# Position bias of a selected-attention kernel: three parts as 48 columns, eighths of a key tile, most steps on ScalarE as plus/minus one

## The chip, the cores and the metric

The kernel runs on one core of a Trainium2 chip. The metric is the device time of one execution, in microseconds, from launch to end on that core. Below, PE is TensorE's matmul, PEld its weight load, DVE VectorE, ACT ScalarE, SP the SyncE queue. All sizes are for 512 tokens, in float32 unless said otherwise.

## What is computed

Two transformer blocks run back to back. The change touches one term of the first block's first attention branch, `dsa_attention`: the bias that is added to the scaled logits by the distance between a query and a key.

```python
def t5_bucket(dist):                       # 32 buckets
    d = jnp.maximum(dist, 0)
    dl = jnp.maximum(d, 16).astype(jnp.float32)
    large = 16 + (jnp.log(dl / 16) / math.log(128 / 16) * 16).astype(jnp.int32)
    return jnp.where(d < 16, d, jnp.minimum(large, 31))
...
bias = rel_bias[t5_bucket(pb[:, :, None] - p_sel)]      # rel_bias: 32 buckets x 4 heads
s = einsum('bthd,btkd->bthk', qb, k_sel) * scale + moveaxis(bias, -1, 2)
s = where(valid, s, -1e30); p = softmax(s)
```

The positions are inputs of the kernel. The 512 queries and 512 keys make a causal 4 x 4 grid of tiles of 128 x 128, of which ten are needed, each for four heads.

## The kernel before

**The whole.** The kernel is one program of some 19,800 instructions without loops on the device; each engine has its own stream, and semaphores tie the streams. In order: projections of the first block, an index score and a top-k selection, a gated recurrence, a latent attention (`mla`), the position bias, the selected attention (`dsa`), the output gates and projections, a feed-forward, and then the second block with its own projections, a state-space part and attention. Weights come through a ring of four slots on the SP queue. Most weight products are made as three float32r products (head by head, head by rest, rest by head; `triple`, L667 to L684), so each tile of weights is rounded by ACT (`weight_heads`, L1289) and its rest subtracted by DVE (`weight_rests`, L1634, called through `tt`, L1740).

**Work that is laid beside other work.** Projection products that nothing needs soon are cut in steps and spread over the stretches in which PE has gaps. `BESIDE` (L133) lists the steps, `PLACES` (L136) the places and how many steps each takes; PE, ACT and DVE each have a function `beside(place)` that runs the steps, drains the finished ones and prepares the coming weights. The last 24 tiles of `BESIDE` are the output gates: one tile is 8 x 3 matmuls of 512 columns, cut in two steps. ACT drains a finished gate tile by Tanh out of PSUM (`drains1`, L1403), and issues its DMA to DRAM on its own queue (L1404). Twelve places `bias 0` to `bias 11` take the last six steps, one in every other place, which are three gate tiles.

**The position bias.** A bucket's bias is a sum of increments: bias(d) is the sum over buckets b, up to the bucket of d, of `rel[b] - rel[b-1]`. So for a group of four keys the 32 bucket limits times 4 keys fill the 128 partitions; a **step** tile says for each (key, limit) and each query whether the query's position is at or past it (0 or 1), and a matmul with the step tile as weights and the increments as the moving operand (16 columns: 4 keys x 4 heads) gives the bias of 128 queries for 4 keys. The increments are split in three bfloat16 parts, `REL[0..2]`, whose products accumulate in PSUM, so that the sum has float32's precision. The steps are written as float32 and read as bfloat16 by taking every second half-word (`STEPS_B`, L417).

`BIAS_PARTS` (L422) goes by key tile: key tile 0 has four query tiles (and so 512 columns of steps), key tile 1 three, 2 two, 3 one. Within a key tile, for each of 32 groups of four keys:

- DVE makes the steps by one `is_ge` of 512, 384, 256 or 128 columns (L1998, recorded as L1743), at most four groups ahead of PE;
- PE makes, for each query tile, three matmuls of 16 columns (L976), each with its own weight load, into the query tile's own PSUM bank;
- after groups 7, 19 and 31 PE comes to a `beside` place.

When all 32 groups are done, DVE adds the mask `chosen` and writes the four heads' bias of each query tile to `BIAS` in SBUF (L2005, 512 columns each). The next key tile's matmuls wait for banks by `BIAS_FREE`. There are 128 DVE steps, 960 small matmuls and 10 of these additions. After the last, PE starts the scores of `dsa` (L815), DVE adds the bias to each score row (L2010) and takes its maximum, and ACT takes the exponential (L1270).

DVE's and ACT's helper `step` makes each instruction wait for the end of the one before.

## Time and profile before

| | |
|---|---|
| runs | 1639.21, 1639.64, 1646.55 us (median 1639.64) |
| the profiled execution | 1639.6 us |
| its span, first to last instruction | 1637.8 us |
| busy: PE / PEld / DVE / ACT / POOL | 1461.7 / 1117.3 / 966.7 / 479.3 / 16.2 us |
| mean granted clock of TensorE (1 is 2.4 GHz) | 0.935 |

The span is shorter than the time by what lies around it, 1.8 us. "Busy" of an engine counts its instructions' time; matmuls are pipelined, so a busy PE is not a PE at its peak. The granted clock is the share of 2.4 GHz that TensorE got; in a short stretch it is 1 or 0.5, and a mean between them says how the stretch was divided. In the groups of instructions a row gives the source line, the engine, the operation, the tiles (out<-in), shapes and count, then busy time in us, mean ns of one, and after the second bar the time for which the engine sat idle before them, with what ended that wait. Line numbers can be those of a helper: `ts` is L1743, `tt` L1740.

### The profile page before, as it was taken

What the parts mean: (1) busy time and instruction counts of PE and PEld (TensorE: products, weight loads), DVE (VectorE), ACT (ScalarE), POOL (GpSimd) and SP (SyncE); (2) the same over time, 40 slices, a digit from 0 to 9 for tenths busy, and PEclk for the clock granted to TensorE, in tenths of its full rate; (3) what the DMA queues carried; (4) which work ended last, traced back from release to release, by engine and by line L of the source; (5) the groups of instructions that cost most, each with busy time, mean ns of one, the idle gap of its engine ahead of it and who ended that gap; (6) DMA issues with size and microseconds to landing.
All of it is one profiled execution on the core that took longest, in us unless ns stands there. A gap on an engine that the chain in (4) does not pass through costs nothing.

```text
span 1637.8 us, 19815 instructions
## 1 busy us (share of the span) xinstructions
PE 1461.7 (89%) x7670; PEld 1117.3 (68%) x7670; DVE 966.7 (59%) x1649; ACT 479.3 (29%) x767; POOL 16.2 (1%) x11
## 2 busy tenths in 40 slices
PE   5998988896899888799899999999798997859998
PEld 4757888784577665687688888888477754446753
DVE  6259767655366767774546645533693648268840
ACT  5256322331322003323423432432213221114410
POOL 0000000000000000000000000000000011000000
PEclk9999999997999778899899999999898999969999
DMA  5112111221222100452134444123321112500001
GB/s 224 65 52 87 55 39 52 90 94 64 90 78 78 41 8 33 152 190 102 71 141 155 167 154 156 53 106 121 94 74 51 64 66 81 203 24 1 1 1 51
DMA packets 39885, 140.56 MB, mean 86 GB/s; under 512 B 13040, under 2 KB 17520, under 8 KB 27248
## 3 DMA queue, kind: packets, MB, share of 16 engines
q1 hardware_dynamic: 34608, 130.52, 22.2%
q10 hardware_dynamic: 5184, 8.78, 1.5%
q8 instruction: 61, 1.00, 0.2%
q14 instruction: 32, 0.26, 0.1%
HBM read 128.41 MB, written 8.39 MB: 84 GB/s over the span
## 4 chain that ended last, share of the span: by engine, by line
PE 53%; DVE 5%; issue 1%; ACT 1%; SPq 1%; DMA 0%; ACTq 0%; DVEq 0%; POOL 0%; POOLq 0%
PE turn L677 22%; PE score L662 7%; PE score L677 5%; PE sum L662 4%; PE turn L662 3%; PE sum L677 2%; PE sum L1205 2%; PE score L1110 1%; PE score L1179 1%; PE turn L1191 1%; SPq L603 1%; PE turn L1083 0%; DVE work L1740 0%; PE score L1236 0%; PE score L1150 0%
## 5 line engine op out<-in xcount | busy, mean ns | idle before, releaser
L1740 DVE TENSOR_TENSOR ring_r<-ring,heads_r 128x1024 fp32r<-128x1024 f32 (+3 forms) x153 | 176.3, 1152 | 216.8 <-ACT heads_r L1289 181.4
L1289 ACT ACTIVATE heads_r<-ring 128x1024 fp32r<-128x1024 f32 (+3 forms) x153 | 153.4, 1002 | 240.8 <-DMA ring<-wstream 103.1
L677 PE MATMUL score<-h_sb_r,heads_r 128*128 128x512 f32 x376 | 152.0, 404 | 0.0
L677 PE MATMUL turn<-tiles_r,heads_r 128*128 128x512 f32 x336 | 132.1, 393 | 0.0
L677 PE MATMUL turn<-h_sb_r,heads_r 128*128 128x512 f32 x304 | 119.5, 393 | 8.1 <-DVE ring_r L1740 8.1
L677 PE MATMUL turn<-wide_r,heads_r 128*128 128x512 f32 x312 | 121.9, 391 | 0.0
L677 PE MATMUL turn<-wide_r,ring_r 128*128 128x512 f32 x312 | 121.6, 390 | 0.0
L677 PE MATMUL score<-x_sb_r,heads_r 128*128 128x512 f32 x256 | 109.5, 428 | 8.2 <-DVE ring_r L1740 5.8
L677 PE MATMUL score<-x_sb_r,ring_r 128*128 128x512 f32 x256 | 104.3, 407 | 0.0
L677 PEld LDWEIGHTS score<-h_sb_r,heads_r 128*128 128x128 f32 x376 | 74.3, 197 | 14.7 <-issue 0.2
L677 PEld LDWEIGHTS turn<-tiles_r,heads_r 128*128 128x128 f32 x336 | 63.9, 190 | 13.3
L677 PEld LDWEIGHTS turn<-h_sb_r,heads_r 128*128 128x128 f32 x304 | 57.7, 190 | 20.4 <-issue 8.4
L677 PEld LDWEIGHTS score<-x_sb_r,heads_r 128*128 128x128 f32 x256 | 51.8, 202 | 23.9 <-issue 10.0
L677 PE MATMUL sum<-h_sb_r,heads_r 128*128 128x512 f32 x168 | 67.6, 403 | 0.0
L677 PEld LDWEIGHTS turn<-wide_r,heads_r 128*128 128x128 f32 x312 | 58.9, 189 | 12.3
L677 PEld LDWEIGHTS turn<-wide_r,ring_r 128*128 128x128 f32 x312 | 58.8, 188 | 12.2
L1258 ACT ACTIVATE tiles<-score 128x512 f32<-128x512 f32 x39 | 24.3, 622 | 143.1 <-PE score L677 73.8
L1743 DVE TENSOR_SCALAR work<-prow,work 128x512 f32<-128x512 f32 (+3 forms) x128 | 49.5, 386 | 19.7 <-PE turn L976 6.2
L677 PEld LDWEIGHTS score<-x_sb_r,ring_r 128*128 128x128 f32 x256 | 51.1, 200 | 11.6
L662 PE MATMUL score<-h_sb,ring 128*128 128x512 f32 x128 | 55.8, 592 | 0.0
L677 PE MATMUL turn<-h_sb_r,ring_r 128*128 128x512 f32 x128 | 50.3, 393 | 0.0
L677 PE MATMUL score<-wide_r,heads_r 128*128 128x512 f32 x120 | 47.3, 394 | 2.6 <-DVE h_sb_r L1740 2.6
(398 smaller groups left out, 2912.0 us busy)
## 6 DMA issues: line engine op xcount, KB each, us to landing
ring<-wstream SPq DMA_DIRECT2D x95, 1024.0 KB, 4.9
ring<-wstream SPq DMA_DIRECT2D x16, 704.0 KB, 4.3
ring<-gated SPq DMA_DIRECT2D x6, 1024.0 KB, 7.0
gated<-tiles ACTq DMA_DIRECT2D x15, 256.0 KB, 2.7
gated<-probs ACTq DMA_DIRECT2D x9, 256.0 KB, 2.0
x_sb<-xT SPq DMA_DIRECT2D x4, 512.0 KB, 5.7
x_sb<-xT ACTq DMA_DIRECT2D x1, 2048.0 KB, 8.1
outT<-x_sb SPq DMA_DIRECT2D x1, 2048.0 KB, 6.3
```

The costliest lines, as they stand in the source:

```text
L603: sp.dma_start(tiles[32 * r:32 * r + 32, 14 * T:18 * T].rearrange("p (k a m) -> p k a m", k=4, a=STEP)[:, :, m, :], U4[32 * m:32 * m + 32, ...
L662: mm = pe.matmul(out, l, r, start=(i == 0), stop=(i == len(pairs) - 1))
L677: return pe.matmul(out, a, w, **k) if moving else pe.matmul(out, w, a, **k)
L1110: mm = pe.matmul(b[0:2 * NCMP, 0:256], CB[kv][:, 8 * i + l, :], w[:, l, :], start=(i + l == 0), stop=(8 * i + l == 31))
L1179: pe.matmul(PAIR[p % 2][:, e * T:e * T + cols], TL[r, 18 + j, n * P:(n + 1) * P], KT2[r, 2 * a_ + j // 2, 0:cols], start=True, stop=False)
L1191: mm = pe.transpose(b[:, j * P:(j + 1) * P], PROB(i)[:, j * P:(j + 1) * P], ident)
L1205: mm = pe.matmul(OUT[g][:, h % 4 * P:h % 4 * P + P], PROBT(i)[:, j * P:(j + 1) * P], R2[:, j, at_v:at_v + P], start=(j == 0), stop=(j == n))
L1258: step(act.activation(out, b, func, bias=bias, scale=scale), name, gemm_done)
L1289: step(act.activation(head_piece(p), chunk(name)[:, c:c + cols], ACT.Identity), f"head {p}")
L1740: step(dve.tensor_tensor(out, a, b, op), name)
L1743: step(dve.tensor_scalar(out, a, s1, s2, o1, *([o2] if o2 is not None else [])), name)
```

## The change

The bias is cut in 32 **eighths** (`EIGHTHS`: key tile, eighth), four groups of four keys each, in the order of the key tiles.

- The three bfloat16 parts of the increments stand side by side in 48 columns. One matmul per step tile and query tile gives the three products, unsummed, in three places 64 columns apart of a PSUM bank. Two query tiles share a bank (192 of each 256 columns used); even eighths use the two `score` banks, odd ones the two `turn` banks. PE waits, before eighth i, for the additions of eighth i-2.
- Of each four groups, DVE makes the steps of the first as before; ACT makes the other three as Sign(position - limit + 0.5), plus or minus one, written as bfloat16 into a ring of eight tiles `SIGNS`. For these the increments are halved, with the last bucket's bias put to bucket 0 as the constant (`rel_last`, a new small input of 16 columns), so `REL` has two versions.
- DVE sums the three parts and the mask itself: for each pair of query tiles three dependent additions (`both` gives the view of two query tiles at once), 128 elements per partition for a pair, 64 for a single one.
- The increments' preparation, on DVE, goes from 10 to 18 small instructions, and a tile `KEYSIGN` is made of `KEYSTEP`, both ahead of them.
- The three gate tiles are cut into 24 steps of one k (three matmuls) each, one after each of the eighths 4 to 27. The places are six, at the eighths 4, 8, 12, 16, 20 and 24: there ACT drains finished gate tiles and rounds weights, and DVE subtracts rests.

```diff
@@ -135,7 +135,7 @@
          [("rows1_cq1", n) for n in range(NT)] + [(f"proj1c_{i // 4}", i) for i in range(4, 2 * len(PROJ1C))] + [(f"gate_{i // 4}", i) for i in range(2 * len(GATES))]
 PLACES = [(f"rank {i}", 2) for i in range(8)] + [(f"rec {h} {l}", 1) for h in range(4) for l in range(LEVELS + 1)] + \
          [(f"tail {i}", 2) for i in range(4)] + [("latent 0", 2), ("latent 1", 4)] + [(f"mla {i}", 1) for i in range(18)] + \
-         [(f"bias {i}", 1 - i % 2) for i in range(12)]
+         [(f"bias {i}", 1) for i in range(6)]
 PLACE = {n: i for i, (n, _) in enumerate(PLACES)}
 assert sum(k for _, k in PLACES) == len(BESIDE)
@@ -260,6 +260,10 @@
         for j in range(4):
             m[j, shift:, j, :] = a["rel_bias"][0:32 - shift]
         c[name] = m.reshape(P, 16)
+    m = np.zeros((4, 32, 4, 4), np.float32)
+    for j in range(4):
+        m[j, 0, j, :] = a["rel_bias"][31]
+    c["rel_last"] = m.reshape(P, 16)
     for kv in "kv":
         pos = a[f"cmp_pos_{kv}_2"][0].T
         c[f"pos_{kv}"] = np.concatenate([pos, pos], 0)
@@ -408,21 +412,33 @@
     BIAS = part(wide, 0, 5120, k=4)
     INDEX = [None] + [part(work, n * T, (n + 1) * P) for n in range(1, NT)]
     RANKED = [None, INDEX[1], INDEX[2], TL[:, 4, :]]
-    REL = [part(work, 6 * T + 8 * z, 8).bitcast(BF16) for z in range(3)]
-    KEYSTEP = part(work, 6 * T + 64, P)
-    def STEPS(g, cols):
-        return part(work, (2 + g % 4) * T, cols)
-    def STEPS_B(g, e):
-        return part(work, (2 + g % 4) * T + e * P, P).bitcast(BF16)[:, 1:2 * P:2]
-    BIAS_PARTS = [(0, (0, 1, 2, 3), (S[0], S[1], U[0], U[1])), (1, (1, 2, 3), (O[0], S[0], S[1])),
-                  (2, (2, 3), (U[0], U[1])), (3, (3,), (O[0],))]
-    BIAS_FREE = [0, 2, 4, 5]
+    REL = [part(work, 6 * T + 24 * v, 24).bitcast(BF16) for v in range(2)]
+    KEYSTEP, KEYSIGN = part(work, 6 * T + 64, P), part(work, 6 * T + 192, P)
+    STEP_OF = {g: ("act", "dve")[g % 4 == 0] for g in range(32)}
+    EIGHTHS = [(key, o) for key in range(NT) for o in range(8)]
+    BIAS_BANKS = [[S[0], S[1]], [U[0], U[1]]]
+    def STEPS(i):
+        return part(work, (2 + i % 2) * T, T)
+    def SIGNS(n):
+        return part(work, (7 * T, 4 * T)[n // 4 % 2] + n % 4 * 256, 256).bitcast(BF16)
+    def both(v, n, lo, count):
+        s = (n + 1) * P
+        x = max(0, lo + 2 * s - v.shape[-1])
+        if count == 1:
+            return v[:, :, lo:lo + 16].unsqueeze(1)
+        return v[:, :, lo - x:lo - x + 2 * s].rearrange("p h (e s) -> p e h s", e=2)[:, :, :, x:x + 16]
     LOGITS = [part(work, 4 * T, T), part(work, 5 * T, T)]
+    def signs_of(i, g):
+        return 3 * i + g % 4 - 1
     def upto(n):
@@ -692,7 +708,7 @@
                     at_c = c + k * P
                     last = any(c0 + k_ == at_c + P for _, c0, k_ in piece_of[name])
                     mm = triple(out, name, at_c, P, ah, ar, k == 0, k == n - 1, last)
-                    if halves and k == n // 2 - 1:
+                    if k < n - 1 and halves and (halves == "each" or k == n // 2 - 1):
                         yield
                 yield mm
@@ -706,7 +722,7 @@
                 for i, c in list(enumerate(by_twos(tiles_)))[first:last]:
                     for e in range(len(c)):
                         b = gemm_bank()
-                        for mm in split_tile(b[:, :], f"{tag}_{i}", e * KD * P, acts, None, True):
+                        for mm in split_tile(b[:, :], f"{tag}_{i}", e * KD * P, acts, None, "each" if tag == "gate" and 2 * i + e >= 21 else True):
                             if mm is None:
                                 yield
                         mm.then_inc(gemm_full, 1)
@@ -966,20 +982,24 @@
             pe.wait_ge(turn_done, tally.count["turn_full"])
             pe.wait_ge(score_done, tally.count["score_full"])
             pe.wait_ge(sum_done, sums[0])
-            for c_, (key, queries, banks) in enumerate(BIAS_PARTS):
-                if c_:
-                    pe.wait_ge(bias_done, BIAS_FREE[c_])
-                for g in range(32):
-                    pe.wait_ge(dve_step, at(f"steps {c_} {g}"))
-                    for e, b in enumerate(banks):
-                        for z in range(3):
-                            mm = pe.matmul(b[:, 16 * g:16 * g + 16], STEPS_B(g, e), REL[z],
-                                           start=(z == 0), stop=(z == 2))
-                    mm.then_inc(steps_used if g < 31 else bias_full, 1)
-                    up(steps_used if g < 31 else bias_full, f"bias {c_} {g}")
-                    if g % 12 == 7:
-                        beside(f"bias {3 * c_ + g // 12}")
-            pe.wait_ge(bias_done, 10)
+            for i, (key, o) in enumerate(EIGHTHS):
+                if i >= 2:
+                    pe.wait_ge(bias_done, i - 1)
+                for g in range(4 * o, 4 * o + 4):
+                    by_act = STEP_OF[g] == "act"
+                    pe.wait_ge(*((act_step, at(f"signs {i} {g}")) if by_act else (dve_step, at(f"steps {i} {g}"))))
+                    for e in range(NT - key):
+                        if by_act:
+                            l = SIGNS(signs_of(i, g))[:, e * P:(e + 1) * P]
+                        else:
+                            l = STEPS(i)[:, e * P:(e + 1) * P].bitcast(BF16)[:, 1:2 * P:2]
+                        dst = BIAS_BANKS[i % 2][e // 2][:, e % 2 * 256:e % 2 * 256 + 192].rearrange("p (z c) -> p z c", z=3)
+                        mm = pe.matmul(dst[:, :, g % 4 * 16:g % 4 * 16 + 16], l, REL[by_act].rearrange("p (z c) -> p z c", z=3),
+                                       start=True, stop=True)
+                    mm.then_inc(signs_used if by_act else steps_used, 1)
+                if 4 <= i < 28:
+                    run(units, 1)
+            pe.wait_ge(bias_done, len(EIGHTHS))
             attention("dsa", 4, lambda h: [TL[:, 13 + h, :]], lambda h: [TL[:, 17, :]],
                       lambda h, j: ROW[:, j, 0:128], P, masked=False)
@@ -1453,8 +1473,17 @@
             attention_exp("mla", 4, beside=lambda i: beside(f"mla {i}"))
             for i in (16, 17):
                 beside(f"mla {i}")
-            for i in range(12):
-                beside(f"bias {i}")
+            act.wait_ge(dve_step, at("key signs"))
+            for i, (key, o) in enumerate(EIGHTHS):
+                if 4 <= i < 28 and i % 4 == 0:
+                    beside(f"bias {i // 4 - 1}")
+                for g in range(4 * o, 4 * o + 4):
+                    if STEP_OF[g] == "act":
+                        n = signs_of(i, g)
+                        if n >= 8:
+                            act.wait_ge(signs_used, n - 7)
+                        step(act.activation(SIGNS(n)[:, 0:T - key * P], prow[:, key * P:].bitcast(F32), ACT.Sign,
+                                            bias=KEYSIGN[:, 32 * key + g:32 * key + g + 1]), f"signs {i} {g}")
             drains(units_before(len(PLACES)))
             attention_exp("dsa", 4, lambda i, cols: LOGITS[i % 2][:, 0:cols])
@@ -1984,26 +2013,46 @@
             stt(SILU_C, SILU_C, 1.0, sm("c2"), ALU.add, ALU.mult)
             ts(SILU_C, SILU_C, 0.5, None, ALU.mult, name="silu c")
             inc, rest = stat[:, 64:80], stat[:, 80:96]
-            tt(inc, sm("rel"), sm("rel_before"), ALU.subtract)
-            for z in range(3):
-                step(dve.tensor_copy(REL[z], inc), "increments" if z == 2 else None)
-                step(dve.tensor_copy(rest, REL[z]))
-                tt(inc, inc, rest, ALU.subtract)
             ts(KEYSTEP, pkey[:, :].bitcast(F32), con("least"), None, ALU.add)
-            for c_, (key, queries, banks) in enumerate(BIAS_PARTS):
-                t0, t1 = queries[0] * P, (queries[-1] + 1) * P
-                for g in range(32):
-                    if g >= 4:
-                        dve.wait_ge(steps_used, at(f"bias {c_} {g - 4}"))
-                    ts(STEPS(g, t1 - t0), prow[:, t0:t1].bitcast(F32), KEYSTEP[:, 32 * key + g:32 * key + g + 1], None, ALU.is_ge,
-                       name=f"steps {c_} {g}")
-                    if g % 12 == 7:
-                        beside(f"bias {3 * c_ + g // 12}")
-                dve.wait_ge(bias_full, c_ + 1)
-                for n, b in zip(queries, banks):
-                    lo = upto(n) + key * P
-                    step(dve.tensor_tensor(BIAS[:, :, lo:lo + P], b[:, :].rearrange("p (s h) -> p h s", h=4),
-                                           chosen[:, lo:lo + P].unsqueeze(1).broadcast_to([P, 4, P]), ALU.add), None, bias_done)
+            ts(KEYSIGN, KEYSTEP, -1.0, 0.5, ALU.mult, ALU.add, name="key signs")
+            for v in range(2):
+                tt(inc, sm("rel"), sm("rel_before"), ALU.subtract)
+                if v:
+                    tt(inc, inc, sm("rel_last"), ALU.add)
+                    ts(inc, inc, 0.5, None, ALU.mult)
+                for z in range(3):
+                    out = REL[v][:, 16 * z:16 * z + 16]
+                    step(dve.tensor_copy(out, inc), "increments" if (v, z) == (1, 2) else None)
+                    if z < 2:
+                        step(dve.tensor_copy(rest, out))
+                        tt(inc, inc, rest, ALU.subtract)
+            def steps(i):
+                key, o = EIGHTHS[i]
+                for g in range(4 * o, 4 * o + 4):
+                    if STEP_OF[g] == "dve":
+                        if i >= 2:
+                            dve.wait_ge(steps_used, i - 1)
+                        ts(STEPS(i)[:, 0:T - key * P], prow[:, key * P:].bitcast(F32), KEYSTEP[:, 32 * key + g:32 * key + g + 1], None,
+                           ALU.is_ge, name=f"steps {i} {g}")
+            steps(0)
+            for i, (key, o) in enumerate(EIGHTHS):
+                if 4 <= i < 28 and i % 4 == 0:
+                    beside(f"bias {i // 4 - 1}")
+                if i + 1 < len(EIGHTHS):
+                    steps(i + 1)
+                dve.wait_ge(signs_used, 3 * (i + 1))
+                for n in range(key, NT, 2):
+                    lo, count = upto(n) + key * P + 16 * o, min(2, NT - n)
+                    parts_ = BIAS_BANKS[i % 2][(n - key) // 2].rearrange("p (e c) -> p e c", e=2)[:, 0:count, 0:192]
+                    parts_ = parts_.rearrange("p e (z t h) -> p z e h t", z=3, h=4)
+                    dst = both(BIAS, n, lo, count)
+                    mask = both(chosen[:, :].unsqueeze(1), n, lo, count).broadcast_to([P, count, 4, 16])
+                    tt(dst, parts_[:, 0], mask, ALU.add)
+                    tt(dst, parts_[:, 1], dst, ALU.add)
+                    step(dve.tensor_tensor(dst, parts_[:, 2], dst, ALU.add), None, bias_done if n + 2 >= NT else dve_step)
             def biased(i, n, h, src):
                 out = LOGITS[i % 2][:, 0:(n + 1) * P]
```

## Rows read from the trace of the kernel before

**Rows 1.** The page: the span's busy time by engine.

```profile
PE 1461.7 (89%) x7670; PEld 1117.3 (68%) x7670; DVE 966.7 (59%) x1649; ACT 479.3 (29%) x767; POOL 16.2 (1%) x11
```

**Rows 2.** Busy time by stretch: the bias, the selected attention, then up to 1400 us.

```profile
core 0: us, PE busy (x) PEld busy (x) DVE busy (x) ACT busy (x) POOL busy (x), PEclk, DMA share, GB/s
538.00:619.00 81.00, 67.87 (x1033) 52.31 (x1033) 58.76 (x140) 2.85 (x4) 0.00 (x0) 0.69 0.10 31
619.00:690.00 71.00, 56.36 (x272) 42.10 (x273) 55.71 (x96) 25.64 (x52) 0.00 (x0) 0.87 0.19 68
```

**Rows 3.** Groups of instructions between 538 and 619 us, shapes kept apart.

```profile
L1743 DVE TENSOR_SCALAR work<-prow,work 128x512 f32<-128x512 f32 x32 | 15.6, 486 | 4.1 <-PE turn L976 3.0
L1743 DVE TENSOR_SCALAR work<-prow,work 128x384 f32<-128x384 f32 x32 | 13.4, 420 | 5.1 <-PE score L976 4.0
L1743 DVE TENSOR_SCALAR work<-prow,work 128x256 f32<-128x256 f32 x32 | 11.3, 353 | 4.3 <-PE turn L976 3.2
L1743 DVE TENSOR_SCALAR work<-prow,work 128x128 f32<-128x128 f32 x32 | 9.2, 286 | 6.1 <-PE sum L976 5.0
...
L976 PEld LDWEIGHTS turn<-work 128*128 128x128 bf16 x384 | 14.6, 102 | 8.6 <-DVE work L1743 4.0 <-DVE wide L2005 2.8 <-issue 0.3
...
L1740 DVE TENSOR_TENSOR ring_r<-ring,heads_r 128x1024 fp32r<-128x1024 f32 x2 | 2.5, 1226 | 0.1
```

**Rows 4.** Timeline of DVE where the bias begins (start us, duration us).

```profile
535.53 0.17 DVE L1740 TENSOR_TENSOR stat<-sml 128x16 f32<-128x16 f32 x1
535.74 0.17 DVE L1989 CAST work<-stat 128x16 bf16<-128x16 f32 x1
...
537.62 0.29 DVE L1743 TENSOR_SCALAR work<-pkey,cst 128x128 f32<-128x128 f32 x1
537.95 1.01 DVE L1743 TENSOR_SCALAR work<-prow,work 128x512 f32<-128x512 f32 x2
```

**Rows 5.** Timeline where the bias ends and the attention begins.

```profile
618.10 0.69 DVE L2005 TENSOR_TENSOR wide<-sum,chosen 128x512 f32<-128x512 f32 x1 [0.41 <-PE sum L976]
...
618.84 1.22 PE L815 MATMUL score<-tiles 128*128 128x128 f32 x4 [0.85 <-DVE wide L2005]
```

**Rows 6.** Timeline of ACT around the first gate tile drained within the bias.

```profile
563.14 0.60 ACT L1258 ACTIVATE tiles<-sum 128x512 f32<-128x512 f32 x1 [27.52 <-PE sum L677]
563.76 0.33 ACTq L1404 DMA_DIRECT2D gated<-tiles  x1
564.14 1.06 ACT L1289 ACTIVATE heads_r<-ring 128x1024 fp32r<-128x1024 f32 x1 [0.40 <-ACT tiles L1258]
```

**Rows 7.** Groups of ACT, whole span: activations with a bias operand, and a table load.

```profile
L1549 ACT ACTIVATE work<-work,cst 128x512 f32<-128x512 f32 x4 | 2.9, 722 | 0.1
L1270 ACT ACTIVATE probs<-work,stat 128x384 f32<-128x384 f32 x4 | 2.5, 615 | 6.1 <-issue 6.1
L1270 ACT ACTIVATE probs<-work,stat 128x256 f32<-128x256 f32 x4 | 2.0, 507 | 5.7 <-issue 4.8 <-ACT probs L1270 0.9
...
L1270 ACT ACTIVATE probs<-work,stat 128x128 f32<-128x128 f32 x4 | 1.6, 402 | 7.0 <-DVE stat L1718 6.2 <-ACT probs L1270 0.8
...
L1270 ACT ACT_TABLE_LOAD x1 | 1.3, 1283 | 17.3 <-DVE stat L1718 17.3
```

**Rows 8.** Groups of DVE, whole span: small additions.

```profile
L1740 DVE TENSOR_TENSOR stat<-stat 128x16 f32<-128x16 f32 x14 | 2.4, 175 | 0.5
...
L1740 DVE TENSOR_TENSOR work<-score,wide 128x128 f32<-128x128 f32 x4 | 1.2, 292 | 1.5 <-PE score L815 1.3
```

**Rows 9.** Timeline of PE: small matmuls and gate matmuls at the low, then the full clock.

```profile
540.05 0.33 PE L976 MATMUL score<-work 128*128 128x16 bf16 x6
540.24 0.31 PE L976 MATMUL turn<-work 128*128 128x16 bf16 x6
...
543.05 0.63 PE L677 MATMUL sum<-h_sb_r,heads_r 128*128 128x512 f32 x1
543.48 0.63 PE L677 MATMUL sum<-x_sb_r,ring_r 128*128 128x512 f32 x1
...
545.48 0.39 PE L677 MATMUL sum<-h_sb_r,heads_r 128*128 128x512 f32 x1
545.71 0.39 PE L677 MATMUL sum<-x_sb_r,ring_r 128*128 128x512 f32 x1
```

More of the change, by code:

```diff
@@ L288 @@
 SMALL = {"g_attn": 8, "g_ffn": 8, "g_final": 8, "g_cq": 3, "g_ckv": 2, "g_ob": 1, "g_2": 8, "b_ada": 24, "c2": 8,
-         "glu_b": 4, "ssm_d": 16, "rel": 16, "rel_before": 16, "g_q": 64, "g_kc": 64, "g_ks": 64, "g_kw": 64, "pos_k": 32, "w2_k": 128,
+         "glu_b": 4, "ssm_d": 16, "rel": 16, "rel_before": 16, "rel_last": 16, "g_q": 64, "g_kc": 64, "g_ks": 64, "g_kw": 64, "pos_k": 32, "w2_k": 128,
          "pos_v": 32, "w2_v": 128, "a_re": 16, "a_im": 16, "log_dt": 16}
@@ L515, in two_blocks_kernel @@
     sum_full, sum_done = sem("sum_full"), sem("sum_done")
-    steps_used, bias_full, bias_done = sem("steps_used"), sem("bias_full"), sem("bias_done")
+    signs_used, steps_used, bias_done = sem("signs_used"), sem("steps_used"), sem("bias_done")
     heads_used, cmp_used = sem("heads_used"), sem("cmp_used")
```

## The prediction, made before the changed kernel was run

> **What bounds the kernel now.** I read the page's busy shares first [rows 1]: PE 89%, DVE 59%, ACT 29%. That mean says nothing of the stretch that the change touches, so next the busy time by stretch [rows 2]. The bias takes 81.0 us; in it PE counts as busy 67.9, DVE 58.8 and ACT only 2.9, at a mean clock of 0.69. The groups of that stretch [rows 3] show who waits. DVE's steps are busy 15.6 + 13.4 + 11.3 + 9.2 = 49.5 us, and ahead of them DVE is idle for 4.1 + 5.1 + 4.3 + 6.1 = 19.6 us, most of it until PE. PE in turn waits for DVE's steps (the idle time of its weight loads). So they alternate: in most of the stretch DVE's 128 steps set the pace, and at each `beside` place a half gate tile, 12 matmuls of 0.43 us at the low clock [rows 9] or 5.1 us, outlasts the four groups that DVE may be ahead (4 x 0.52), and DVE stands still. ACT, idle, could do steps; and gate products in small pieces would stop nobody. Nothing else runs on the path meanwhile: the first score waits for the last addition, which ends at 618.79 [rows 5].
>
> **The change, part by part.** I work out when the last addition ends; the rest of the kernel should shift by the difference. Prices are of one instruction with the wait for its end, which costs about 0.03 us (the second step tile starts 0.52 us after the first, of 0.486 [rows 3, 4]).
>
> *Preparation.* Before, the increments start at 535.53 and the first step at 537.95 [rows 4]. After, `KEYSTEP` and `KEYSIGN` (0.32 each) come first, so ACT may begin at about 536.2; then 18 small instructions 0.21 us apart [rows 4], 3.7 us: the first step starts at 539.9. That is 2.0 us lost, all on DVE.
>
> *Steps by DVE.* 8 per key tile, at 0.52, 0.45, 0.39 and 0.32: 13.4 us instead of 53.7.
>
> *Additions by DVE.* Ten of 0.69 (7.2 with gaps) become 144 small ones. A pair of query tiles is 128 elements: 0.292 + 0.033 = 0.325 [rows 8]. A single one, 64, lies between the 0.175 of 16 elements and the 0.292 of 128: an estimate of 0.225 + 0.033 = 0.258. An eighth of key tile 0 has six of 0.325, of key tile 1 three and three, of 2 three of 0.325, of 3 three of 0.258. With its step, an eighth costs DVE 2.47, 2.20, 1.36 and 1.09 us; eight of each are 57.0 us. The weight rests, 2 x 1.25, stay [rows 3].
>
> *Signs by ACT.* Each has a bias operand from SBUF. Such activations took 0.722, 0.615, 0.507 and 0.402 us by width [rows 7]; the lower bound is 0.631 for 512 columns, the 0.60 us drain without that operand [rows 6] plus the gap. I take the first. Three per eighth: 2.27, 1.94, 1.62, 1.31 us, 57.1 in all. So the 40 us taken off DVE's steps cost ACT 57, and ACT and DVE come out equal.
>
> The Trainium skill speaks against this move: "ScalarE: Activation LUTs", section "Rules for kernel authors", says to use VectorE and not ScalarE for max, add and the like. The trace agrees on the single instruction, 0.722 against 0.486 us [rows 3, 7]; by that rule the stretch would gain nothing. But it counts an instruction, and here ACT is idle for 78 of 81 us [rows 2].
>
> *Matmuls.* 960 become 320 of 48 columns. At the low clock two groups of six 16-column matmuls start 0.19 apart, 0.032 each, and 512 columns take 0.43, which scaled to 48 is 0.040 [rows 9]. I take 0.040. Bounds: 0.032, and 0.10 if each weight load (0.102 [rows 3]) stood alone. An eighth with its gate piece (3 x 0.43 = 1.28) keeps PE for 1.9, 1.8, 1.6 and 1.4 us: under DVE in key tiles 0 and 1, level with ACT in 2 and 3. At full clock (0.23 per gate matmul [rows 9]) PE is far below both.
>
> *Gate tiles.* The work is unchanged, 72 matmuls. It is hidden behind DVE's additions now, since PE may be one eighth ahead. What is new is a meeting of ACT and PE. At eighths 12 and 20 ACT, before it makes that eighth's signs, waits for PE to end the gate tile whose last piece stands behind eighth 11 (19), drains it (0.63), issues its DMA on its own queue (0.4 until it goes on) and at 12 rounds a weight piece (1.09) [rows 6]. All signs of eighth 12 are queued behind this wait, PE waits for them, and DVE for PE. ACT's lead of eight signs is gone there. At eighth 4 the same work (2.1 us) finds its tile long done and is covered by that lead. The SP queue's loads into the ring are moved earlier with the gate tiles, and nothing near reads them.
>
> **The sum** (low clock). DVE from 539.9: first step 0.5, eighths 0 to 10 take 8 x 2.47 + 3 x 2.20 = 26.4, one rest 1.25, which gives 568.1; PE ends the gate tile behind eighth 11 at about 568.5. ACT: + 0.2 latency + 2.1 = 570.8. Signs for 12 to 19, which nothing else holds up: 4 x 1.94 + 4 x 1.62 = 14.2, 585.0. DVE at 12 to 15 keeps that pace to 581.4, then a rest and three eighths of 1.36 bring it to 586.8, and PE ends the gate tile behind 19 at 588.0. ACT drains by 589.2 (no rounding). Signs for 20 to 31 in one go: 4 x 1.62 + 8 x 1.31 = 16.9, 606.1. Last matmuls and three additions: 1.1, so 607.2. Against 618.8 that is 11.6 us less. Full clock throughout gives 605.0 in the same walk. I take the low clock, since the stretch had 0.69 with three times the small matmuls.
>
> After it, `dsa` is DVE's (55.7 of 71.0 us busy [rows 2]) and starts in both cases behind a thin piece of PE work, so I add nothing. The profiled execution took 1639.6, its own span 1637.8 and 1.8 around it; 1639.6 - 11.6 = 1628.0. The median of the runs is the same 1639.6.
>
> **Bounds.** Full clock with ACT at the lower price: 601.8, or 1622.6. Matmuls at 0.104: 616.1, or 1636.9. Additions 10% dearer, 609.6, or 1630.4.
>
> **The rivals.** *Weight loads do not overlap at 48 columns*, and PE at 16 x 0.104 + 1.28 = 2.9 us per eighth takes the place of DVE: 1636.9. Against it: at 16 columns 12 matmuls went through in 0.38 us [rows 9]. Chance 0.09.
>
> *Sign lies in another function table than Tanh and Exp.* Then ACT loads tables around each gate drain, at 1.28 us [rows 7]. Two of the drains are on the path (eighths 12 and 20), two loads each, 5.1 us, and about 1 to 2 more at the start and end: 1634.5. For it: three activation lines of this kernel pay such loads. Against it: Identity runs between Tanh and Exp in the stretch before without one. Chance 0.07. The Trainium skill, "ScalarE: Activation LUTs", section on table sets, puts the cheap functions in every set but does not name Sign with Tanh; it gives 2.7 us for a switch, where the row has 1.28 and decides.
>
> *DVE's small additions cost more than their size says* (four-dimensional views, runs of 16, PSUM read four elements apart). Nothing is gained if a pair costs 0.46 instead of 0.325 (the price of 256 elements, 0.424 + 0.033): 1640, chance 0.09. Slower than before is this mechanism further on: at 0.55 and 0.43 DVE needs 3.8 us per eighth of key tile 0, ends at 630.5, and the time is 1651; it decides from 0.52 on. Against both: the old additions read PSUM with the same stride of four, at 0.69 for 512 elements [rows 5]. Chance 0.06.
>
> **How the numbers follow.** My case, 1625.5 to 1631.4, has 0.69. A measurement of this kernel can tell about 0.5% (8.2 us) from no change. Faster than 1631.4: my case, 0.69. Within 0.5%: the loads, the tables, the first form of the dear additions and small misses, 0.25. Slower than 1647.8: 0.06. The range that holds 8 in 10 goes from 1623.0 (near the lower bound) to 1636.5.
>
> **What would show it.** In the changed profile: DVE's small additions near 0.29 and 0.23 us; signs at 0.72 to 0.40 with no table load among them; the stretch from the first step to the first score about 67 us instead of 81; ACT busy some 57 us more; two pauses of DVE of 2 to 3.5 us behind the second and third drained gate tile; the 48-column matmuls 0.03 to 0.04 apart. I am wrong if DVE waits for PE in key tiles 0 and 1, if the signs leave 0.75 us for 512 columns, or if the stretch is shorter and a later one longer, above all `dsa` through a colder clock.

## The result, and the profile after

| | before | after |
|---|---|---|
| runs | 7 | 7 |
| median (lowest to highest), us | 1644.26 (1639.21 to 1648.37) | 1634.97 (1632.83 to 1636.64) |
| profiled execution / its span | 1639.6 / 1637.8 | 1635.3 / 1633.5 |
| clock, mean over the span | 0.935 | 0.932 |

The ratio of the times is 0.9943, 95% interval 0.9927 to 0.9958: faster by 0.57%, 9.3 us on the medians, where 11.6 were forecast. 1634.97 lies inside the range 1623.0 to 1636.5 and 7 us above the forecast of 1628.0. Further sets of runs of the kernel before had medians of 1643.0 to 1646.5; the profiled execution on which the sum was made, 1639.6, was among its fastest.

The page after, its busy shares, against [rows 1]:

```profile
PE 1447.7 (89%) x7030; PEld 1103.2 (68%) x7030; DVE 963.1 (59%) x1696; ACT 533.2 (33%) x863; POOL 16.2 (1%) x11
```

ACT has 54 us more, PE 640 instructions and 14 us less; the shares hardly tell that anything happened. So the bias by itself: busy time from the first step to the end of the last addition, first after, then in a second profile of the kernel before (its first had 80.9 us in this cut, PE 67.7, DVE 58.8, ACT 2.85 busy, against [rows 2]).

```profile
core 0: us, PE busy (x) PEld busy (x) DVE busy (x) ACT busy (x) POOL busy (x), PEclk, DMA share, GB/s
543.00:609.60 66.60, 44.54 (x392) 29.01 (x392) 53.48 (x178) 54.88 (x98) 0.00 (x0) 0.73 0.14 44
```

```profile
539.70:623.10 83.40, 70.47 (x1032) 53.82 (x1032) 58.77 (x140) 2.85 (x4) 0.00 (x0) 0.64 0.09 27
```

DVE and ACT are each busy for over 80% of the stretch; before, DVE and PE took turns in it and ACT was idle. The stretch, 66.6 us, is 14.2 us shorter than in the first profile of before. Its groups after, between 536 and 630 us, answer to [rows 3] (steps), [rows 7] (signs) and [rows 8] (additions):

```profile
L1485 ACT ACTIVATE work<-prow,work 128x512 bf16<-128x512 f32 x24 | 17.3, 722 | 9.2 <-DVE work L1772 8.4
L1485 ACT ACTIVATE work<-prow,work 128x384 bf16<-128x384 f32 x24 | 14.8, 615 | 0.8
L1485 ACT ACTIVATE work<-prow,work 128x256 bf16<-128x256 f32 x24 | 12.2, 508 | 1.2 <-ACT tiles L1278 0.4
...
L1485 ACT ACTIVATE work<-prow,work 128x128 bf16<-128x128 f32 x24 | 9.6, 402 | 0.8
...
L1769 DVE TENSOR_TENSOR wide<-score,chosen 128x128 f32<-128x128 f32 x16 | 4.7, 291 | 5.4 <-PE score L997 5.0
L1769 DVE TENSOR_TENSOR wide<-turn,chosen 128x128 f32<-128x128 f32 x16 | 4.7, 291 | 1.5 <-PE turn L997 1.0
...
L1772 DVE TENSOR_SCALAR work<-prow,work 128x512 f32<-128x512 f32 x8 | 3.9, 486 | 0.3
...
L1769 DVE TENSOR_TENSOR wide<-score,chosen 128x64 f32<-128x64 f32 x8 | 1.8, 224 | 0.7 <-PE score L997 0.5
...
L1769 DVE TENSOR_TENSOR wide<-turn,chosen 128x64 f32<-128x64 f32 x8 | 1.8, 224 | 1.0 <-PE turn L997 0.8
```

The prices of ACT's and DVE's instructions are met within 1 ns: signs 722, 615, 508, 402, additions 291 and 224 (estimated 225), steps 486. DVE's idle time ahead of its steps, 19.6 us in [rows 3], is down to 1.2; what it still waits for PE is 7.3 us, all ahead of the first addition of an eighth (5.0 + 1.0 + 0.5 + 0.8). The timeline shows it, DVE above, ACT below:

```profile
573.84 0.42 DVE L1772 TENSOR_SCALAR work<-prow,work 128x384 f32<-128x384 f32 x1
576.56 0.29 DVE L1769 TENSOR_TENSOR wide<-score,chosen 128x128 f32<-128x128 f32 x1 [2.30 <-PE score L997]
...
593.69 0.29 DVE L1769 TENSOR_TENSOR wide<-score,chosen 128x128 f32<-128x128 f32 x1 [1.69 <-PE score L997]
```

```profile
572.10 0.60 ACT L1278 ACTIVATE tiles<-sum 128x512 f32<-128x512 f32 x1 [4.79 <-PE sum L693]
572.72 0.33 ACTq L1424 DMA_DIRECT2D gated<-tiles  x1
573.10 1.06 ACT L1309 ACTIVATE heads_r<-ring 128x1024 fp32r<-128x1024 f32 x1 [0.40 <-ACT tiles L1278]
574.18 14.23 ACT L1485 ACTIVATE work<-prow,work 128x384 bf16<-128x384 f32 x24
590.68 0.60 ACT L1278 ACTIVATE tiles<-score 128x512 f32<-128x512 f32 x1 [2.27 <-PE score L693]
```

ACT stands idle for 4.8 us until PE ends the gate tile behind eighth 11, then drains it, issues its DMA and rounds weights, and makes signs only from 574.18 on. DVE, which needs them by way of PE, has nothing to do from 574.3 to 576.56. Behind eighth 19 it is the same, with 2.3 us of idle time on ACT and 1.7 on DVE.

**Why the whole gained less than the stretch.** By the two first profiles: the first step comes 5.1 us later after the change (543.02 against 537.95 in [rows 4]). Of these, 1.9 are the longer preparation, and 3.1 lie ahead of it: the preparation itself begins at 538.68 instead of 535.53. The stretch gives 14.2 back; from the last addition to the end of the span there are 1019.0 us before and 1023.9 after, 4.9 more, in code that the change leaves alone. In sum that is 4.3 us, the difference of the two spans. Two places hold most of the 4.9. The first is from the read-back of x to the first feed-forward gate, the second from the last feed-forward gate to the second block's norm. Before, then after:

```profile
657.40:800.50 143.10, 128.08 (x543) 104.07 (x543) 94.83 (x130) 46.49 (x58) 0.00 (x0) 0.93 0.37 133
1022.90:1169.40 146.50, 137.65 (x620) 113.52 (x618) 60.99 (x94) 49.44 (x71) 0.00 (x0) 0.96 0.29 100
```

```profile
648.10:792.50 144.40, 129.37 (x542) 105.41 (x543) 94.86 (x130) 46.50 (x59) 0.00 (x0) 0.92 0.37 131
1014.90:1164.30 149.40, 140.55 (x620) 116.25 (x618) 61.00 (x94) 49.42 (x71) 0.00 (x0) 0.94 0.29 98
```

DVE and ACT are busy for the same time within 0.1 us; only PE takes longer, at a lower granted clock (0.92 for 0.93, 0.94 for 0.96). Whether the change does this is what the experiments on repeats and delays ask.

### The profile page after: what moved, and what is told of

It reads as the page before. It is cut to its first block, busy times and chain, and to the rows that moved or that the text cites. A ratio compares the mean times of both kernels' runs of the same rounds, so it can differ in the third digit from the quotient of the medians.

```text
span 1633.5 us, 18739 instructions
## 1 busy us (share of the span) xinstructions
PE 1447.7 (89%) x7030; PEld 1103.2 (68%) x7030; DVE 963.1 (59%) x1696; ACT 533.2 (33%) x863; POOL 16.2 (1%) x11
## 4 chain that ended last, share of the span: by engine, by line
PE 53%; DVE 5%; issue 1%; ACT 1%; SPq 1%; DMA 0%; ACTq 0%; DVEq 0%; POOL 0%; POOLq 0%
PE turn L693 22%; PE score L678 7%; PE score L693 5%; PE sum L678 4%; PE turn L678 3%; PE sum L693 2%; PE sum L1225 2%; PE score L1130 1%; PE score L1199 1%; PE turn L1211 1%; SPq L619 1%; PE turn L1103 0%; PE turn L1046 0%; DVE work L1769 0%; PE score L1256 0%
## 5 line engine op out<-in xcount | busy, mean ns | idle before, releaser
L693 PEld LDWEIGHTS turn<-wide_r,ring_r 128*128 128x128 f32 x312 | 58.8, 188 | 12.4
L693 PEld LDWEIGHTS score<-x_sb_r,ring_r 128*128 128x128 f32 x256 | 51.2, 200 | 11.6
L1485 ACT ACTIVATE work<-prow,work 128x512 bf16<-128x512 f32 (+3 forms) x96 | 53.9, 562 | 11.9 <-DVE work L1772 8.4
L1638 ACT ACTIVATE tiles<-score,stat 128x128 f32<-128x128 f32 (+3 forms) x64 | 33.7, 527 | 51.1 <-issue 40.0
```

The source lines that it names most:

```text
L693: return pe.matmul(out, a, w, **k) if moving else pe.matmul(out, w, a, **k)
L1485: step(act.activation(SIGNS(n)[:, 0:T - key * P], prow[:, key * P:].bitcast(F32), ACT.Sign, bias=KEYSIGN[:, 32 * key + g:32 * key + g + 1] ...
L1638: step(act.activation(PROB(i)[:, 0:cols], PAIR[p % 2][:, i % 2 * T:i % 2 * T + cols], ACT.Exp, bias=stat[:, 8 + i % 4:9 + i % 4], scale=1. ...
```

## The experiments

"Stretch" is from the first step to the end of the last addition; the kernel before has 80.8 and 83.4 us, the changed one 66.6. "The two stretches behind" are the two just shown. The experiments were measured in three groups, each together with new runs of the kernel before. Its medians were 1642.99 us (beside repeats, late drains, and the version with everything together), 1646.49 (beside steps without ACT, two of four, the 48 columns undone and six blocks) and 1646.09 (beside the delays, the second profile of late drains, and the version together without late drains). Where "one run" stands, there is no interval, and the stretch in its profile is the evidence.

**Repeats.** Both kernels again, unchanged.

> The kernel before, unchanged, for a second profile. In the first pair of profiles the bias stretch (first preparation instruction to the end of the last addition) is 12.2 us shorter after the change, but the whole span only 4.3: 3.1 us are lost ahead of the stretch and 4.8 behind it, in places that the change does not touch, each time with a slightly lower granted clock. Theory (chance of the clock): a second profile of the same kernel moves by some us in these places too, while its bias stretch stays at 81 us within 1.5. Rival (the change cools the clock elsewhere): the old kernel repeats its first profile within 0.5 us in each stretch outside.

> The changed kernel, unchanged, for a second profile. Theory (chance): stretch from the first step to the end of the last addition 66.6 us within 1.5, as in the first; the stretches outside move by 1 to 3 us in sum. Rival: they again stand 8 us behind those of the kernel before.

Before: 1644.08 us in one run, stretch 83.4 (0.9 beyond what was expected; its clock was 0.64 against 0.69), first step 1.7 later than in its first profile, and the two stretches behind 143.0 and 146.4. After: 1634.62 (1632.79 to 1637.61) against 1642.99, ratio 0.9950 (0.9934 to 0.9967); stretch 66.6, the two behind 144.3 and 149.3. So neither theory holds as it stood: what lies ahead of the bias moved by 1.7 us between the two profiles of the kernel before (0.2 in the changed one), but the two stretches behind have in both profiles of a kernel the same length within 0.1. By the two second profiles the change gives 16.8 us in the stretch and loses 3.2 ahead of the first step and 4.6 behind the last addition, 9.0 in all, about what the medians give.

**Late drains.** The gate tiles are drained four eighths later, the weights rounded without waiting.

```diff
-                if 4 <= i < 28 and i % 4 == 0:
-                    beside(f"bias {i // 4 - 1}")
+                if i == 4:
+                    beside("bias 0")
+                if i == 12:
+                    weight_heads(upto=pieces_through(PLACE["bias 4"]))
+                if i in (16, 24):
+                    drains(units_before(PLACE[f"bias {i // 4 - 2}"]))
```

> The changed kernel, but ACT drains the gate tiles of the eighths 11 and 19 four eighths later (at 16 and 24), and rounds the weight piece at 12 without a wait. Theory (the meeting of ACT and PE empties ACT's lead and costs two pauses of DVE): the pauses of 2.3 and 1.7 us behind the eighths 11 and 19 and the short ones of 0.5 after them go; first step to last addition from 66.6 to 61 to 62.5, time 4 to 5.5 us under the changed kernel. Rival (DVE waits there because PE is slow, not because signs are late): no change within 1 us.

> The version with late drains again, for a second profile. First step to last addition 61.6 us within 0.5; outside it the same lengths as its first profile if they go with the kernel (as in the two profiles of the changed kernel), others of the same small set if they go by the run.

Stretch 61.6 in both profiles: 5.0 gained, as the theory had it. ACT no longer waits for PE at a drain; within the stretch it waits for PE only where it needs a free sign tile:

```profile
565.62 1.06 ACT L1309 ACTIVATE heads_r<-ring 128x1024 fp32r<-128x1024 f32 x1
...
574.48 0.60 ACT L1278 ACTIVATE tiles<-sum 128x512 f32<-128x512 f32 x1
575.11 0.33 ACTq L1424 DMA_DIRECT2D gated<-tiles  x1
...
583.06 1.59 ACT L1489 ACTIVATE work<-prow,work 128x256 bf16<-128x256 f32 x3 [1.66 <-PE turn L997]
```

The meeting of ACT and PE is shown as the cause of the pauses. The time fell further, to 1625.94 (1622.63 to 1628.01), ratio 0.9896 (0.9877 to 0.9914): 8.7 us under the changed kernel's 1634.62 of the same group, where 4 to 5.5 were expected; the run of the second profile took 1626.73. The 3.7 beyond the stretch lie outside it: the two stretches behind are 142.8 and 146.8 in both profiles, 4.0 less than in the changed kernel, the first step comes 0.7 to 1.7 earlier, and what follows the second stretch takes 1.2 longer.

**A delay behind the selected attention.** One or three multiplications on DVE's path, with nothing else changed.

```diff
             step(dve.memset(stat[:, 60:61], 0.0), "dsa done")
+            for _ in range(1):      # 3 in the second
+                tt(part(work, T, T), con("level")[:, 0:T], con("level")[:, 0:T], ALU.mult)
```

> The changed kernel with one idle DVE multiplication of 512 columns (0.72 us with its wait) put on the path behind the selected attention. In the profiles so far, the stretches behind the bias that the change does not touch come out in a few discrete lengths: from the last feed-forward gate to the second block's norm 146.5, 149.4 or 150.6 us, from the read-back of x to the first feed-forward gate 143 or 144.4, each with a granted clock to match. Theory (where a burst of PE work begins against the clock's own changes is chance, and shifts with everything ahead): the delay moves some of them to another of these lengths, so that the time changes by something else than 0.7 us, between -4 and +4. Rival (the longer stretches belong to the change): all stay as in the changed kernel within 0.3 us, and the time is 0.7 longer.

> The same with three such multiplications (2.17 us). Theory: lengths from the same small set, the time changes by between -3 and +5 us. Rival: plus 2.2 us, all other stretches within 0.3.

With 0.72 us added the time was 1632.04 (1629.89 to 1636.00), ratio 0.9916 (0.9896 to 0.9936); with 2.17 added 1633.49 (1629.89 to 1633.73), ratio 0.9922 (0.9906 to 0.9939). Without, the ratios were 0.9943 and 0.9950, with intervals that overlap these: the runs do not show that the added work makes the whole faster, but they do not show it 0.7 or 2.2 us slower either. From the last feed-forward gate on, by pieces, with the delay and without (the changed kernel):

```profile
1013.30:1159.90 146.60, 137.75 (x620) 113.58 (x618) 61.05 (x94) 49.45 (x72) 0.00 (x0) 0.95 0.30 100
1013.30:1023.30 10.00, 10.00 (x69) 9.10 (x67) 5.11 (x7) 6.63 (x11) 0.00 (x0) 1.00 0.23 72
1023.30:1033.30 10.00, 10.00 (x40) 8.25 (x41) 9.52 (x15) 8.70 (x14) 0.00 (x0) 0.83 0.01 2
```

```profile
1014.90:1024.90 10.00, 10.00 (x57) 9.10 (x56) 5.08 (x7) 6.62 (x11) 0.00 (x0) 0.87 0.23 72
1024.90:1034.90 10.00, 10.00 (x37) 8.62 (x38) 9.52 (x15) 7.96 (x13) 0.00 (x0) 0.62 0.01 2
```

In the first 20 us the mean clock was 1.00 and then 0.83 in the one, 0.87 and then 0.62 in the other, and the stretch is 146.6 or 149.4 (three multiplications: 146.7). From the last addition to the end there are 1020.4 and 1020.9 us; less the added work, 1019.7 and 1018.7, against 1023.9 without it and 1019.0 before the change. The second stretch moved to another of the lengths seen before, as the theory had it, and the code there is the same: the 4.9 us are not a fixed price of the change.

The delay does not show by itself what gives them back. Both profiles are of the fastest of four runs, one for each kernel, and they differ from the changed kernel already ahead of the added work, where the code is the same: the first step stands at 541.12 and 539.74 instead of 543.02. The first of the two stretches stays long, 144.6 and 145.2 with the added work in it.

(The steps of the changed kernel and of the one with one multiplication, with the start of the first and of the last:)

```profile
L1772 DVE TENSOR_SCALAR work<-prow,work x32: 286/387/487, 543.0 to 607.1; 128x512 f32<-128x512 f32 x8, 128x384 f32<-128x384 f32 x8, 128x256 f32<-128x256 f32 x8, 128x128 f32<-128x128 f32 x8
L1772 DVE TENSOR_SCALAR work<-prow,work x32: 286/387/487, 541.1 to 605.1; 128x512 f32<-128x512 f32 x8, 128x384 f32<-128x384 f32 x8, 128x256 f32<-128x256 f32 x8, 128x128 f32<-128x128 f32 x8
```

Nor does the moment counted from the start of the span decide. The kernel before came to the second stretch at 1022.9 us in one profile and at 1027.4 in the other and took 146.5 and 146.4; with late drains it was 1006.9 and 1007.7, and 146.8 both times. So the lengths repeated for each of the three kernels that were profiled twice, which is more than the run's chance that I had supposed; what sets them stays open.

**Steps without ACT.**

```diff
-    STEP_OF = {g: ("act", "dve")[g % 4 == 0] for g in range(32)}
+    STEP_OF = {g: ("act", "dve")[g % 4 in (0, 1, 2, 3)] for g in range(32)}
...
-        return part(work, (2 + i % 2) * T, T)
+        return part(work, (2, 3, 4, 5, 7, 8)[n % 6] * T, T)
```

> The changed kernel with all steps made by DVE and none by ACT (ring of six step tiles). Theory (DVE's steps and additions add up on one engine): 53.7 + 43.6 + 2.5 = 99.8 us from the first step to the last addition, so 33 us over the changed kernel and some 20 over the one before. Rival (PE or ACT was the bound, DVE had room): under 80.

```profile
542.20:642.30 100.10, 66.97 (x392) 38.03 (x392) 90.61 (x274) 2.85 (x4) 0.00 (x0) 0.52 0.09 30
```

Stretch 100.1, DVE busy 90.6 of it and the rest the short gaps between its instructions; the time was 1668.57 in one run, against 1646.49. Without ACT's share the rest of the change (48 columns, eighths, fine gate pieces) would have been a loss of 22 us.

**Two of four steps by DVE**, rings of four: `STEP_OF` with `g % 4 in (0, 2)`.

> The changed kernel with two of four steps by DVE and two by ACT (rings of four step and four sign tiles). Theory (DVE bounds key tiles 0 and 1; the ratio of 3 to 1 balances the engines): DVE needs 26.8 + 43.6 + 2.5 = 73 us, first step to last addition 73 to 74, 7 over the changed kernel. Rival (ACT bounds it all): shorter than 66.6.

Stretch 74.0, as expected, and 1640.12 us in one run. In it DVE waits for PE for 0.9 us in all, ACT for free sign tiles and gate tiles for over 30: with two steps of four and three additions for each pair, DVE is the bound, in all four key tiles and not only in 0 and 1.

**The 48 columns undone**, the three parts summed by PE.

```diff
-                        dst = BIAS_BANKS[i % 2][e // 2][:, e % 2 * 256:e % 2 * 256 + 192].rearrange("p (z c) -> p z c", z=3)
-                        mm = pe.matmul(dst[:, :, g % 4 * 16:g % 4 * 16 + 16], l, REL[by_act].rearrange("p (z c) -> p z c", z=3),
-                                       start=True, stop=True)
+                        dst = BIAS_BANKS[i % 2][e // 2][:, e % 2 * 256:e % 2 * 256 + 64]
+                        for z in range(3):
+                            mm = pe.matmul(dst[:, g % 4 * 16:g % 4 * 16 + 16], l, REL[by_act][:, 16 * z:16 * z + 16],
+                                           start=(z == 0), stop=(z == 2))
...
-                    tt(dst, parts_[:, 0], mask, ALU.add)
-                    tt(dst, parts_[:, 1], dst, ALU.add)
-                    step(dve.tensor_tensor(dst, parts_[:, 2], dst, ALU.add), None, bias_done if n + 2 >= NT else dve_step)
+                    step(dve.tensor_tensor(dst, parts_[:, 0], mask, ALU.add), None, bias_done if n + 2 >= NT else dve_step)
```

> The changed kernel with the 48 columns undone: three accumulating matmuls of 16 columns, and one DVE addition in place of three. DVE is relieved of 29 us, PE takes 640 more matmuls of about 0.03 us (19 us). Theory: ACT (57 us and the two meetings with PE) is then the bound with PE, 61.5 us at full clock, 71 at the low one: within 5 us of the changed kernel either way, so the 48 columns as such are not what gains. Rival (48 columns bring the gain by relieving PE): 75 or more.

```profile
539.70:604.10 64.40, 54.39 (x1032) 41.92 (x1032) 27.76 (x82) 54.85 (x98) 0.00 (x0) 0.74 0.14 46
```

Stretch 64.4, 2.2 less than with the 48 columns, and 1634.18 us (1633.14 to 1635.26), ratio 0.9931 (0.9912 to 0.9950). DVE's busy time halves, and it now waits 34.6 us for PE; ACT's busy time is the same 54.9, and the end hardly moves: ACT is the bound. The 48 columns by themselves gain nothing.

**Gate products in six blocks** of four pieces: `if 4 <= i < 28 and i % 4 == 3: run(units, 4)`.

> The changed kernel with the gate pieces in six blocks of 12 matmuls (behind the eighths 7, 11, 15 and so on), as before the change, in place of 24 pieces of three. Theory (a block of 12 outlasts the one eighth that PE may be ahead, and DVE stands still): 70 us from the first step to the last addition at full clock, 82 at the low one, against 66.6. Rival (only the sum of PE's work counts): 67 or less.

Stretch 77.8, between the 70 and 82 of the theory, and 1644.20 us in one run. DVE's three longest pauses, in its timeline:

```profile
579.89 0.29 DVE L1769 TENSOR_TENSOR wide<-score,chosen 128x128 f32<-128x128 f32 x1 [5.81 <-PE score L997]
...
599.25 0.29 DVE L1769 TENSOR_TENSOR wide<-score,chosen 128x128 f32<-128x128 f32 x1 [3.72 <-PE score L997]
...
609.38 0.23 DVE L1769 TENSOR_TENSOR wide<-score,chosen 128x64 f32<-128x64 f32 x1 [4.00 <-PE turn L997]
```

So the stretch is 11.2 us longer without the fine cut of the gate products. This and the 33.5 us of ACT's share are each measured against the whole change; they do not add up to its gain of 14.2.

**Together**: parts summed by PE, steps two and two, with late drains and without.

> Late drains as before, and besides: the three parts are summed by PE again (three accumulating matmuls of 16 columns in place of one of 48, DVE one addition in place of three), and DVE makes two of four steps in place of one, ACT two in place of three. DVE then has about 27 + 15 + 2.5 us of work, ACT 38 + 5, PE 960 small matmuls. Theory (DVE and ACT bound the changed kernel, PE has room): first step to last addition 48 us at full clock, 64 at the low one where PE is the bound; between them 50 to 62, time 5 to 15 us under the changed kernel. Rival (small matmuls are dear on PE, which is why 48 columns gain): 66 or more, no gain over the changed kernel.

> The fastest version without the late drains: parts summed by PE, steps two and two, ACT and PE meeting at the eighths 12 and 20 as in the changed kernel. Theory: ACT has less to do there (two signs of 0.65 or 0.54 per eighth), so each meeting costs 2 to 3 us: first step to last addition 53 to 56 us against 49.7 with late drains. Rival (PE is the bound of this version and covers the meetings): 49 to 51.

With late drains: stretch 49.7 and 1618.64 us (1615.78 to 1620.71) against 1642.99, ratio 0.9855 (0.9834 to 0.9877), 16 us under the changed kernel of the same group, of which late drains alone gave 8.7, and the fastest of all. Without: stretch 56.2, 0.2 above the theory's 53 to 56, so the rival of 49 to 51 falls and late drains are worth 6.5 us here; 1625.26 us (1624.16 to 1627.46), ratio 0.9874 (0.9858 to 0.9890). The first one's stretch:

```profile
540.10:589.80 49.70, 46.71 (x1032) 37.73 (x1032) 40.12 (x114) 37.60 (x66) 0.00 (x0) 0.87 0.14 46
```

PE 46.7, DVE 40.1 and ACT 37.6 of 49.7: PE, busy for 94% of the stretch, is now the bound, and the other two are not far from it. Its granted clock is 0.87 where the changed kernel had 0.73 with PE busy for 67%, and so the stretch came out near the full-clock end of what was expected. Why the clock was higher was not tested.

## Why the prediction was nearly right

- **Preparation**, 1.9 us longer for the 2.0 of the sum: the first step stands 4.34 us behind the start of `KEYSTEP` (538.68 to 543.02), as worked out (0.64 + 3.7).
- **Steps, additions, signs**: met, as shown above. Making all steps on DVE cost 33.5 us more, the size that the sum gives (99.8 forecast, 100.1 measured).
- **Matmuls**, 0.040 each at the low clock: sixteen of 48 columns span 0.80 to 0.83 us with the last one's own 0.206, so 0.040 to 0.042 each. The rival of weight loads that do not overlap falls. The two groups:

```profile
554.57 0.83 PE L997 MATMUL turn<-work 128*128 128x48 bf16 x16
...
557.04 0.80 PE L997 MATMUL score<-work 128*128 128x48 bf16 x16 [0.19 <-DVE work L1772]
```

- **The two meetings of ACT and PE**: where they were forecast, behind the eighths 11 and 19. DVE's pauses were forecast as 2 to 3.5 us; they are 2.3 and, a little short of it, 1.7. Moving the drains gave back 5.0.
- **The sum for the stretch**: last addition forecast 67.3 us behind the first step, measured 66.6. In the walk, 581.4 does not follow from ACT's pace, as the words have it (570.8 and four eighths of 1.94 give 578.6), but from DVE's own: four of 2.20, begun when the signs of eighth 12 are there.
- **Table loads**: none stands among the signs. The rival falls, and that the time came out near its 1634.5 is coincidence. The prediction read too few loads in the kernel before: not three but fourteen activation lines have one or more, 21 loads in all. Its 1.28 us is the load's own duration; since no load fell among the signs, no run here prices a whole switch.
- **The instruction rule.** The Trainium skill ("ScalarE: Activation LUTs", "Rules for kernel authors") names max and add, not a comparison. If the steps are counted with them, they belong on VectorE by it, and for one instruction the trace agrees (486 ns against 722 at 512 columns); for the kernel, putting them back on VectorE made the stretch 33.5 us longer.
- **Dear additions**: fall too, at 291 and 224 ns.

The step that failed is "so I add nothing" behind the bias. It looked at `dsa` alone, and was right on it: from the last addition to the last exponential there are 32.5 us before and 32.4 after. But 4.9 us were lost further on, where PE had a lower granted clock, 1.3 and 2.9 of them in the two stretches shown. That a later stretch could be longer through a colder clock stands among the prediction's signs of being wrong, but the sum has no term for it.

The sum likewise has no term ahead of the preparation, where the first pair of profiles differs by 3.1 us. The sum for the profiled execution closes with it: 11.6 forecast, less 3.1 ahead and 4.9 behind, plus 0.7 in the stretch and 0.1 in the preparation, is 4.4 us; measured are 4.3, from 1639.6 to 1635.3. In the fourteen profiles the preparation begins between 535.35 and 538.68 us, behind the same work in all changed versions. The changed kernel's own two are the latest of them, and a version of it (the 48 columns undone) is the earliest, 0.2 ahead of the kernel before's first. So these 3.1 us are no fixed price of the change either, and why they differ is open.

The other error is of the base: the profiled execution of before was 4.7 us under the median of its seven runs. Against 1644.26, 11.6 us less would be 1632.7; measured were 1635.0. The range held because its ends had been set by other terms, not because the loss behind was in it. The low clock that the sum took throughout fitted the stretch's 0.73 well enough: the same walk at full clock gives 65.1.

## What to carry to other kernels

Price a change on the stretch where it acts, engine by engine, and then ask what stands in one queue: a drain that waits for TensorE, placed ahead of ScalarE's signs, cost 5 us beside a gain of 14, and nothing but its place was wrong. Work is dear or cheap by which engine is idle, not by the instruction: 57 us on an idle ScalarE beat 40 on a full VectorE. Giving the sums back to TensorE and a step back to VectorE, so that the three engines are more equally busy, shortened the stretch from 66.6 to 56.2 us, and with late drains from 61.6 to 49.7. A change of half a per cent meets differences of 3 to 5 us in places that it leaves alone, at another granted clock. A second profile of both kernels shows which of them repeat; a small delay shows whether such a place must be slow behind the change, but compare the profiles ahead of the delay too, before it is given the credit.

## What the runs showed of the hardware that was not expected

The granted clock in a long busy stretch of unchanged code differs from kernel to kernel and repeats for a kernel. The second stretch behind took 149.4 and 149.3 us in the two profiles of the changed kernel, 146.5 and 146.4 in those of the kernel before, and 146.8 twice with late drains, while the moments at which the stretch began lay 0.1, 4.5 and 0.8 us apart within a pair. All steps on DVE and two of four had 150.6 both, at moments 28.5 us apart. So neither chance alone nor the moment since the start of the span decides; what does is not known. Two profiles of a kernel are few: the runs of the kernel before spread from 1639.21 to 1649.05 us, and its two profiled executions lie 4.4 apart.
